# First attention regrouped: four units a step, the transposes of a group together with side work between them

## The chip, the cores and the metric

The kernel runs on one core of a Trainium2 chip. TensorE (PE, with its weight loads shown as PEld) multiplies, VectorE (DVE) and ScalarE (ACT) do the elementwise work, GpSimd (POOL) and SyncE (SP) only start transfers here. The metric is the device time of one execution, in microseconds (us). All matrices are float32. Products of weights are made of three passes over a high and a low part (`w_hi`, `w_lo`, made on ACT and DVE from each slab of weights).

## The reference

The program is a chain of three layers on 512 positions of width 1024: two blocks of a mixer and an MLP, then a hybrid layer. The change lies in the first mixer alone, a block-causal attention with 16 heads of 64:

```python
q, k, v = jnp.split(h @ w_in, 3, axis=-1)
q = rms_norm(q.reshape(B, S, A_HEADS, A_HEAD_DIM), q_gain) * (A_HEAD_DIM ** -0.5)
k = rms_norm(k.reshape(B, S, A_HEADS, A_HEAD_DIM), k_gain)
...
s = jnp.einsum('bihd,bjhd->bhij', qc, kb).astype(jnp.float32) + bias
s = jnp.where(valid[None, None, None, :], s, -jnp.inf)
p = jax.nn.softmax(s, axis=-1).astype(vb.dtype)
return jnp.einsum('bhij,bjhd->bihd', p, vb)
...
return o @ w_out
```

## The kernel before

Queries are cut in four tiles of 128. A **unit** is one head `h` and one query tile `it`; it sees the 128 x (`it`+1) positions up to its own tile, so its scores are 128, 256, 384 or 512 wide. There are 64 units, and two heads (a head pair) have eight: `it` = 0, 0, 1, 1, 2, 2, 3, 3. Each goes through this chain:

- PE scores (L651), two units back to back, into one of three PSUM banks;
- DVE adds the bias, negates and takes the row's extreme (L2016) into `a_p` and `neg_max`;
- ACT takes the exponential and the row sum (L1235);
- DVE takes the reciprocal (L2025) and scales (L2027), for two units at once;
- PE transposes the 128x128 tiles of `a_p` (L660) into bank 3 or 4;
- ACT copies them to `a_pt` (L1229);
- PE multiplies by the values (L674), two units at once, into bank 5 or 6; four such products finish the head pair `i`.

Every engine walks the same counter `s`, one unit a step: scores of unit `s`, transposes of unit `s`-6, values of unit `s`-8. On PE the order in a step is scores, transposes, values, then side work. All buffers have eight slots, `a_pt` four.

**Side work.** PE has other products to do meanwhile: the last two panels of `v` (heads 8 to 15), eight uses of 24 matmuls of 256 columns (L476), each in two bursts of 12, in bank 7, copied to `a_v` by ACT (L1209). They take slabs 10 and 11. A slab of weights is split by ACT (`w_hi`, L1088), which waits until PE has used the slab before the last, and then by DVE (`w_lo`, L1517), which waits for ACT. The slab after them (index 12, the first of the output projection) is split in step 26; the side use that frees its buffer ends in step 21. At the end of the attention PE runs the first six of the eight parts of the first output tile (`first_out`) between the last units.

**Finished head pairs.** The first four (`A_EARLY`) are copied to `a_oT` by DVE (L2036), and split to `h_hi` (ACT, L1240) and `h_lo` (DVE, L2031) in steps 41 to 44 and one step later. The last four are split straight from PSUM (L1244, L2039). DVE also does eight products of the conditioning (`ada`, L1541) on the way, one in four steps.

Each engine runs its instructions in the order in which they are written; the waits are on semaphores (`s_full`, `s_done`, `e_done`, `p_ready`, `t_full`, `pt_ready`, `o_full`, `hi_done`, `lo_done`).

Of the kernel before, what the change touches and what calls it, by code (L numbers as in the profile page):

```python
# [11 lines left out]
P = 128  # L12
T = 512
# [44 lines left out]
A_ADA = 8  # L58

# [16 lines left out]
def program(nc, I, out, tab_d, tz_d):  # L76
    ctx = ExitStack()
    with ctx:
# [258 lines left out]
        SIDE_A, SIDE_H = Side([0, 8, 14, 20, 26, 30, 34, 38], TT, 2), Side([1, 11, 22, 33, 44, 55], 2, 2)  # L337
        A_BANKS = {0: 2, 2: 1, 4: 0}
        A_OUT = 6
        A_KEPT = [41 + i for i in range(A_EARLY)]  # L340
# [8 lines left out]
        H_READ = len(SIDE_A.starts) + 1 + H_USES.index(SIDE_H.starts[-1]) + 1  # L349
        ZA_READ = len(SIDE_A.starts) + 1 + H_USES.index(SIDE_H.starts[1]) + 1  # L350
        C_COPIED = [len(SIDE_A.starts) + 1 + H_USES.index(step) + 1 for step, (i, part) in CMP_STEPS.items() if part == 1]
        SIDE_ALL = len(SIDE_A.starts) + 1 + len(H_USES)
# [108 lines left out]
        def _(pe):  # L461
# [179 lines left out]
            def attention_a(score, value, extra):  # L641

                for s in range(NUA + 7):
                    if s < NUA and s % 2 == 0:
                        if s in A_BANKS:
                            pe.wait_ge(sem("acc_free"), c("bank", -A_BANKS[s]))
                        if s >= 2:
                            pe.wait_ge(sem("s_done"), s - 1)
                        for j in range(2):
                            q, k, n = score(UNITS_A[s + j])  # L650
                            last = mm(ps[(s + j) % 3][:, 0:n], q, k, start=True, stop=True)  # L651
                        last.then_inc(sem("s_full"), 1)
                    u = s - 6
                    if 0 <= u < NUA:
                        n = P * (UNITS_A[u][1] + 1)
                        pe.wait_ge(sem("p_ready"), u + 1)
                        if u >= 2:
                            pe.wait_ge(sem("pt_ready"), u - 1)
                        for j in range(0, n, P):
                            last = nc.tensor.transpose(ps[3 + u % 2][:, j:j + P], a_p[:, u % 8, j:j + P], ident[:])  # L660
                        last.then_inc(sem("t_full"), 1)
                    u = s - 8
                    if u >= 0 and s % 2 == 0:
                        h, it = UNITS_A[u]
                        i = h // 2
                        pe.wait_ge(sem("pt_ready"), u + 2)
                        if it == 0 and i >= 2:
                            if i - 2 < A_EARLY:
                                pe.wait_ge(sem("o_kept"), i - 1)
                            else:  # L670
                                pe.wait_ge(sem("xo_lo"), i - 1)
                        for j in range(it + 1):
                            for par in range(2):
                                last = mm(ps[5 + i % 2][HD * par:HD * par + HD, it * P:(it + 1) * P], value(UNITS_A[u + par], j),  # L674
                                          a_pt[:, (u + par) % 4, j * P:(j + 1) * P], start=j == 0, stop=j == it, skip_group_check=True)
                        last.then_inc(sem("o_full"), 1)
                    extra(s)
# [109 lines left out]
            def score_a(u):  # L787
                h, it = u
# [3 lines left out]
            def value_a(u, j):  # L792
                if u in ((8, 0), (12, 0)):
                    pe.wait_ge(sem("side_free"), TT if u[0] == 8 else 2 * TT)
                return a_v[:, j, u[0] * HD:(u[0] + 1) * HD]

            def pair_a(u, k, sl):
                t, cols = u % TT, slice(k * 256, (k + 1) * 256)
                return (ps[7][:, 0:256], (w_hi[sl][:, cols], w_lo[sl][:, cols]),
                        (h_hi[:, k, t * P:(t + 1) * P], h_lo[:, k, t * P:(t + 1) * P]), True)  # L800
# [3 lines left out]
            def first_out(k):  # L804

                sl = c.base("slab") % 2
                if k == 0:
                    pe.wait_ge(sem("s_done"), NUA)
# [690 lines left out]
        def _(dve):  # L1499
# [507 lines left out]
            for s in range(8 * (KT - 1) + 17):  # L2007
# [11 lines left out]
                if SIDE_A.slab(s):  # L2019
                    split()  # L2020
# [485 lines left out]
```

## Time and profile before

| | us |
|---|---|
| median of 3 runs | 1805.32 (1804.76 to 1806.77) |
| span of the profiled execution | 1804.1 |
| first score to last value product | 156.2 to 259.7 |
| PE busy over the span | 1743.7 (97%) |
| DVE busy, ACT busy | 1174.8, 666.0 |

The page has no time of the profiled execution other than its span, from the first to the last instruction; the three times lie 0.7 to 2.7 above it. PE is busy nearly throughout, and the chain of work that ended last is PE for 80% of the span. A busy PE is not one at its peak: a row of the chain of waits gives the time that a block of matmuls held the chain, from its start to the start of what follows.

### The profile page before, as it was taken

The page shows a single profiled execution, that of the slowest core. Times are in us where ns is not written, and L with a number is a line of the kernel's source. Part 1 is how long each engine was busy: PE and PEld are TensorE (multiplying, and loading weights), DVE is VectorE, ACT ScalarE, POOL GpSimd, SP SyncE. Part 2 cuts the span into 40 slices and gives each one's busy share as a digit, 9 for nine tenths or more (in the row PEclk, how much of TensorE's full clock was granted, in tenths as well). Part 3 has the DMA queues.
Part 4 walks back from the last instruction along what each step waited for, and adds up shares of the span by engine and source line. Part 5 has one row for each costly group of instructions (what it writes and reads, how often), then busy time and mean ns, then how long its engine had stood idle before and what let it go on. Part 6 is the DMA issues. An engine that isn't in the chain of part 4 may idle for free.

```text
span 1804.1 us, 24298 instructions
## 1 busy us (share of the span) xinstructions
PE 1743.7 (97%) x9361; PEld 1440.3 (80%) x9361; DVE 1174.8 (65%) x2441; ACT 666.0 (37%) x1081; POOL 101.1 (6%) x194
## 2 busy tenths in 40 slices
PE   4999999999999999999999999999999999989999
PEld 3877769888888888888888898888888887766787
DVE  7778766876376656565454558874687478656564
ACT  4324673523242333233132335232323342366512
POOL 0001100001000100100000000010001100000000
PEclk9999999999999999999999999999999999999999
DMA  9355324335433634652423224354335322300351
GB/s 376 117 184 184 112 72 158 120 138 172 141 117 117 190 119 157 208 181 70 153 81 140 92 84 156 131 167 169 130 138 179 137 94 92 130 36 24 147 193 47
DMA packets 45471, 245.98 MB, mean 136 GB/s; under 512 B 6256, under 2 KB 6480, under 8 KB 27440
## 3 DMA queue, kind: packets, MB, share of 16 engines
q1 hardware_dynamic: 24848, 155.36, 24.0%
q0 software_dynamic: 20512, 89.11, 14.8%
q8 instruction: 74, 1.21, 0.3%
q14 instruction: 37, 0.30, 0.1%
HBM read 229.23 MB, written 15.22 MB: 135 GB/s over the span
## 4 chain that ended last, share of the span: by engine, by line
PE 80%; DVE 12%; ACT 4%; issue 2%; DMA 2%; DVEq 0%; SPq 0%; ACTq 0%
PE ps L476 69%; DVE w_lo L1517 3%; DMA ada_raw<-in_ada 1%; PE ps L840 1%; ACT w_hi L1088 1%; DVE ada_raw L1541 1%; PE ps L973 1%; DVE ada_first L1902 1%; PE ps L651 1%; DVE pre L1634 1%; PE ps L660 1%; PE ps L674 1%; PE ps L962 1%; PE ps L998 1%; PE ps L953 1%
## 5 line engine op out<-in xcount | busy, mean ns | idle before, releaser
L1517 DVE TENSOR_TENSOR w_lo<-w_raw,w_hi 128x2048 fp32r<-128x2048 f32 x136 | 311.6, 2291 | 137.3 <-ACT w_hi L1088 137.1
L1088 ACT ACTIVATE w_hi<-w_raw 128x2048 fp32r<-128x2048 f32 x136 | 260.1, 1913 | 354.3 <-PE ps L476 329.2
L476 PE MATMUL ps<-h_hi,w_hi 128*128 128x512 f32 (+1 forms) x1008 | 378.2, 375 | 5.2 <-DVE w_lo L1517 3.3
L476 PE MATMUL ps<-h_lo,w_hi 128*128 128x512 f32 (+1 forms) x1008 | 372.7, 370 | 0.0
L476 PE MATMUL ps<-h_hi,w_lo 128*128 128x512 f32 (+1 forms) x1008 | 372.5, 370 | 0.0
L476 PEld LDWEIGHTS ps<-h_hi,w_hi 128*128 128x128 f32 x1008 | 190.2, 189 | 39.8 <-issue 4.5
L476 PEld LDWEIGHTS ps<-h_hi,w_lo 128*128 128x128 f32 x1008 | 190.1, 189 | 32.1
L476 PEld LDWEIGHTS ps<-h_lo,w_hi 128*128 128x128 f32 x1008 | 190.3, 189 | 30.2
L476 PE MATMUL ps<-hid_hi,w_hi 128*128 128x512 f32 (+1 forms) x576 | 211.6, 367 | 0.0
L476 PE MATMUL ps<-hid_hi,w_lo 128*128 128x512 f32 (+1 forms) x576 | 210.9, 366 | 0.0
L476 PE MATMUL ps<-hid_lo,w_hi 128*128 128x512 f32 (+1 forms) x576 | 210.9, 366 | 0.0
L476 PE MATMUL ps<-w_hi,h_hi 128*128 128x512 f32 (+1 forms) x480 | 185.9, 387 | 16.2 <-DVE h_lo L1922 9.1
L476 PE MATMUL ps<-w_lo,h_hi 128*128 128x512 f32 (+1 forms) x480 | 183.1, 382 | 0.0
L476 PE MATMUL ps<-w_hi,h_lo 128*128 128x512 f32 (+1 forms) x480 | 182.7, 381 | 0.0
L1541 DVE CUSTOM_DVE_ANT_0 ada_raw<-ada_raw,cond 128x1024 f32<-128x1024 f32 x104 | 126.0, 1222 | 43.0 <-DMA ada_raw<-in_ada 41.9
L476 PEld LDWEIGHTS ps<-hid_lo,w_hi 128*128 128x128 f32 x576 | 108.7, 189 | 17.6
L476 PEld LDWEIGHTS ps<-hid_hi,w_hi 128*128 128x128 f32 x576 | 108.7, 189 | 17.5
L476 PEld LDWEIGHTS ps<-hid_hi,w_lo 128*128 128x128 f32 x576 | 108.7, 189 | 17.4
L476 PEld LDWEIGHTS ps<-w_hi,h_hi 128*128 128x128 f32 x480 | 92.0, 192 | 36.4 <-DVE w_lo L1517 8.2
L397 POOL DMA_DIRECT2D ada_raw<-in_ada x104 | 55.7, 536 | 971.0 <-DVE mod_s L1541 907.0
L476 PEld LDWEIGHTS ps<-w_hi,h_lo 128*128 128x128 f32 x480 | 92.1, 192 | 17.1
L1296 ACT ACTIVATE relu<-ps 128x512 f32<-128x512 f32 x56 | 33.5, 599 | 195.3 <-PE ps L476 195.0
(391 smaller groups left out, 2430.7 us busy)
## 6 DMA issues: line engine op xcount, KB each, us to landing
w_raw<-in_slabs SPq DMA_DIRECT2D x136, 1024.0 KB, 4.8
ada_raw<-in_ada POOLq DMA_DIRECT2D x104, 512.0 KB, 5.1
s_tables<-s_tab POOLq DMA_DIRECT2D x4, 2692.0 KB, 9.2
s_t<-s_tables POOLq DMA_DIRECT2D x4, 2692.0 KB, 9.8
ada_first<-in_ada SPq DMA_DIRECT2D x16, 512.0 KB, 15.1
a_bias<-in_a_bias POOLq DMA_DIRECT2D x16, 256.0 KB, 3.5
xT<-in_xT SPq DMA_DIRECT2D x4, 512.0 KB, 6.2
s_toeplitz<-KTp POOLq DMA_DIRECT2D x32, 64.0 KB, 3.2
```

Of the source, the lines that this page charges most:

```text
L397: gp.dma_start(ada_raw[:, k % 2, :], I["ada"][k]).then_inc(sem(f"ada_in{k % 2}"), 16)
L476: last = mm(o, l, r, start=start and n == 0, stop=stop and n == 2)
L651: last = mm(ps[(s + j) % 3][:, 0:n], q, k, start=True, stop=True)
L660: last = nc.tensor.transpose(ps[3 + u % 2][:, j:j + P], a_p[:, u % 8, j:j + P], ident[:])
L674: last = mm(ps[5 + i % 2][HD * par:HD * par + HD, it * P:(it + 1) * P], value(UNITS_A[u + par], j), a_pt[:, (u + par) % 4, j * P:(j + 1) * ...
L840: last = mm(b[:, t * P:(t + 1) * P], b_v[:, t, gm * P:(gm + 1) * P], b_ws[:, gm // 3, :], start=True, stop=True)
L953: last = mm(ps[(s + g) % 3][:, 0:n], hqr[r, i, ts], hk[r, br - 1, 0:n], start=True, stop=True)
L962: last = nc.tensor.transpose(ps[3 + u % 2][:, j:j + P], h_p[:, u % 8, j:j + P], ident[:])
L1088: A(w_hi[s][:], w_raw[:, s, :], ACT.Copy).then_inc(sem("hi_done"), 1)
L1296: A(relu[:, g % 2, :], b[:], ACT.Relu).then_inc(sem("relu_done"), 1)
L1517: tt(w_lo[s][:], w_raw[:, s, :], w_hi[s][:].bitcast(F32), ALU.subtract).then_inc(sem("lo_done"), 1)
L1541: V.tensor_tensor_reduce(out=w, in0=w, in1=cond[:, which, :], scale=1.0, scalar=0.0, op0=ALU.mult, op1=ALU.add, accum_out=mod_s[:, o:o + 1 ...
```

## The change

The unit of the walk becomes a **group** of four units: two heads, and the query tiles (3, 0) or (2, 1), so each group has the same ten 128x128 tiles. There are 16 groups, and the counter `s` now counts groups, 0 to 18. A step on PE is: scores of both pairs of group `s` (four banks: 4 and 5, 6 and 0); of group `s`-2 the transposes in three rounds r = 0, 1, 2 (unit, unit, and the last two units together, banks 1 and 2 in turn); between rounds 1 and 2 side work (slot 0); side work again (slot 1); then the values of group `s`-3, all into bank 3. The 16 side bursts have fixed places (`A_BURSTS`): three in step 0, three in step 1, two each in steps 2, 3 and 4, one each in 5, 6, 7 and 8, and none after that. `first_out` runs in steps 16 to 18.

ACT copies a round with one instruction, so 48 copies instead of 64, each behind an exponential of the same step. DVE takes one reciprocal for four units. The `ada` products come in steps 2 to 9. The split of slab 12 stands in step 2, the kept head pairs are split in steps 9 to 12 (`A_KEPT`), on ACT at the end of the step and on DVE at the end of the same step.

```diff
+        GROUPS_A = [(h, its) for h in range(0, A_HEADS, 2) for its in ((3, 0), (2, 1))]
+        A_SCORES, A_TURNED, A_O = ((4, 5), (6, 0)), (1, 2), 3
+        A_BURSTS = [(0, 0), (0, 0), (0, 1), (1, 0), (1, 0), (1, 1), (2, 0), (2, 1), (3, 0), (3, 1), (4, 0), (4, 1),
+                    (5, 0), (6, 0), (7, 0), (8, 0)]
+        A_DONE = [A_BURSTS[2 * u + 1][0] for u in range(A_SIDE)]
+        A_FIRST_OUT = [(16, 1), (16, 1), (17, 0), (17, 1), (18, 0), (18, 1)]
+        A_KEPT = [9 + i for i in range(A_EARLY)]
...
     PE:
-                for s in range(NUA + 7):
+                for s in range(NGA + 3):
+                    if s < NGA:
+                        h, its = GROUPS_A[s]
+                        for pair in range(2):
...
+                                pe.wait_ge(sem("s_done"), 4 * s - 2 + 2 * pair)
+                            for par in range(2):
+                                q, k, n = score(h + par, its[pair])
+                                last = mm(ps[A_SCORES[pair][par]][:, 0:n], q, k, start=True, stop=True)
+                            last.then_inc(sem("s_full"), 1)
+                    g = s - 2
+                    if 0 <= g < NGA:
+                        for r in range(3):
+                            v = 3 * g + r
+                            if r == 2:
+                                extra(s, 0)
+                            pe.wait_ge(sem("p_ready"), 4 * g + (1, 2, 4)[r])
+                            if v >= 2:
+                                pe.wait_ge(sem("pt_ready"), v - 1)
...
+                    extra(s, 1)
...
     side use u on PE:
+                    else:
+                        wait(pe, "side_free", u)
...
     ACT:
+                    for q in range(4):
+                        if s < NGA:
+                            act.wait_ge(sem("s_done"), 4 * s + q + 1)
+                            A(p, p, ACT.Exp, ...).then_inc(sem("e_done"), 1)
+                        g = s - 2
+                        if 0 <= g < NGA and q < 3:
+                            act.wait_ge(sem("t_full"), 3 * g + q + 1)
+                            A(a_pt[:, g % 2, p], ps[A_TURNED[(3 * g + q) % 2]][...], ACT.Copy).then_inc(sem("pt_ready"), 1)
+                    for u, done in enumerate(A_DONE):
+                        if done == s:
...
+                            A(a_v[...], ps[A_SPARE[u]][:, 0:256], ACT.Copy).then_inc(sem("side_free"), 1)
+                            if u == TT - 1:
+                                split()
                     if s in A_KEPT:
                         i = A_KEPT.index(s)
                         act.wait_ge(sem("o_kept"), i + 1)
                         A(h_hi[:, i, :], a_oT[:, i, :], ACT.Copy).then_inc(sem("xo_hi"), 1)
     DVE:
+                if s in (0, A_DONE[TT - 1]):
                     split()
+                g = s - 1
+                if 0 <= g < NGA:
+                    dve.wait_ge(sem("e_done"), 4 * g + 4)
+                    step(V.reciprocal(row_inv[:, m], row_sum[:, m]))
+                    for q in range(4):
+                        ts_(p, p, row_inv[:, n:n + 1], None, ALU.mult).then_inc(sem("p_ready"), 1)
-                if s - 1 in A_KEPT:
-                    i = A_KEPT.index(s - 1)
+                if s in A_KEPT:
+                    i = A_KEPT.index(s)
                     dve.wait_ge(sem("xo_hi"), i + 1)
                     tt(h_lo[:, i, :], a_oT[:, i, :], h_hi[:, i, :].bitcast(F32), ALU.subtract).then_inc(sem("xo_lo"), 1)
```

Three places show what stands in a row now. A row names line, operation, tiles and shape; the brackets are the semaphores it waits on.

**PE, a stretch without side work** (late in the stage; `ps` is a PSUM bank). Before, scores, transposes and values of two units alternate:

```order
L651 MATMUL ps0<-a_kT_96,a_qT_95 128x512 [waits s_done]
L651 MATMUL ps1<-a_kT_96,a_qT_95 128x512
L660 MATMUL ps3<-ident_62,a_p_101 128x128 [waits pt_ready,p_ready]
L674 MATMUL ps6<-a_pt_102,a_v_97 64x128 [waits pt_ready]
L674 MATMUL ps6<-a_pt_102,a_v_97 64x128 x7
L660 MATMUL ps4<-ident_62,a_p_101 128x128 [waits pt_ready,p_ready]
L651 MATMUL ps2<-a_kT_96,a_qT_95 128x128 [waits s_done]
L651 MATMUL ps0<-a_kT_96,a_qT_95 128x128
```

Now, from the last round of transposes of step 8 (the last with a side burst) to the first scores of step 9:

```order
L683 MATMUL ps1<-ident_62,a_p_99 128x128 [waits pt_ready,p_ready]
L683 MATMUL ps1<-ident_62,a_p_99 128x128
L702 MATMUL ps3<-a_pt_100,a_v_95 64x128 [waits pt_ready]
L702 MATMUL ps3<-a_pt_100,a_v_95 64x128 x9
L669 MATMUL ps4<-a_kT_94,a_qT_93 128x384 [waits s_done]
```

The four score products of a step follow each other, and the ten value products too; the last round of transposes (bank 1 again) waits for the copy of the first round.

**DVE, the split of slab 12.** Before, it stands between two units, after their scaling:

```order
L2025 RECIPROCAL row_inv<-row_sum 128x2 [waits e_done]
L2027 TENSOR_SCALAR a_p<-a_p,row_inv 128x512 [waits dve_step]
L2027 TENSOR_SCALAR a_p<-a_p,row_inv 128x512
L2016 ISA a_p,neg_max<-ps,a_bias 128x256 [waits t_full,s_full]
L2016 ISA neg_max 128x1
L1517 TENSOR_TENSOR w_lo<-w_raw,w_hi 128x2048 [waits hi_done]
```

Now, in step 2, it stands ahead of the scaling of group 1:

```order
L2074 ISA a_p,soft<-ps,a_bias 128x128
L2074 ISA soft 128x1
L1572 TENSOR_TENSOR w_lo<-w_raw,w_hi 128x2048 [waits hi_done]
L2092 RECIPROCAL soft<-soft 128x4 [waits e_done]
L2095 TENSOR_SCALAR a_p<-a_p,soft 128x384 [waits dve_step]
L2095 TENSOR_SCALAR a_p<-a_p,soft 128x384
L2095 TENSOR_SCALAR a_p<-a_p,soft 128x256 x2
L1596 ISA ada_raw,mod_s<-ada_raw,cond 128x1024 [waits ada_in0]
```

What moved is the wait for `hi_done`: the scaled tiles that PE transposes next in step 3 now come behind it.

**DVE, the low part of a kept head pair.** Before, it stands between the scores of two units:

```order
L2016 ISA a_p,neg_max<-ps,a_bias 128x256 [waits t_full,s_full]
L2016 ISA neg_max 128x1
L2031 TENSOR_TENSOR h_lo<-a_oT,h_hi 128x512 [waits xo_hi]
L2016 ISA a_p,neg_max<-ps,a_bias 128x256 [waits t_full,s_full]
L2016 ISA neg_max 128x1
```

Now, in step 12, it is the last of the step, ahead of all score rows of step 13:

```order
L2092 RECIPROCAL soft<-soft 128x4 [waits e_done]
L2095 TENSOR_SCALAR a_p<-a_p,soft 128x384 [waits dve_step]
L2095 TENSOR_SCALAR a_p<-a_p,soft 128x384
L2095 TENSOR_SCALAR a_p<-a_p,soft 128x256 x2
L2099 TENSOR_TENSOR h_lo<-a_oT,h_hi 128x512 [waits xo_hi]
L2074 ISA a_p,soft<-ps,a_bias 128x384 [waits t_full,s_full]
```

What it waits for (`xo_hi`) is the last instruction of the same step on ACT.

## Rows read from the trace of the kernel before

**Rows 1.** The page's head and first part: span; busy time of an engine.
```profile
span 1804.1 us, 24298 instructions
PE 1743.7 (97%) x9361; PEld 1440.3 (80%) x9361; DVE 1174.8 (65%) x2441; ACT 666.0 (37%) x1081; POOL 101.1 (6%) x194
```

**Rows 2.** Stretch, length, busy PE, PEld, DVE, ACT, POOL; clock, DMA, GB/s.
```profile
156.20:260.40 104.20, 101.19 (x818) 70.15 (x819) 74.23 (x258) 73.56 (x212) 11.83 (x20) 1.00 0.31 104
222.30:250.70 28.40, 27.85 (x230) 16.42 (x230) 23.51 (x91) 25.39 (x78) 2.26 (x4) 1.00 0.19 63
```

**Rows 3.** The chain of waits in the attention: start us, us, what.
```profile
199.82 0.59 PE ps L660 x4
...
201.80 1.06 PE ps L651 x4
202.86 0.26 PE ps L660
203.12 1.02 PE ps L674 x16
204.15 1.63 PE ps L476 x12
205.78 0.11 PE ps L660
205.89 1.43 PE ps L476 x12
207.31 0.42 PE ps L651 x4
...
208.10 0.37 PE ps L674 x4
```

**Rows 4.** Timeline of ACT: start us, us, engine, line, operation, [idle before].
```profile
238.48 0.60 ACT L1229 ACTIVATE a_pt<-ps 128x512 f32<-128x512 f32 x1 [0.20 <-PE ps L660]
238.98 0.60 ACT L1235 ACTIVATE a_p<-a_p,neg_max 128x384 f32<-128x384 f32 x1
...
240.29 0.72 ACT L1235 ACTIVATE a_p<-a_p,neg_max 128x512 f32<-128x512 f32 x1 [0.20 <-DVE neg_max L2016]
...
241.26 0.71 ACT L1235 ACTIVATE a_p<-a_p,neg_max 128x512 f32<-128x512 f32 x1
...
241.96 0.58 ACT L1244 ACTIVATE h_hi<-ps 128x512 fp32r<-128x512 f32 x1
...
243.51 0.40 ACT L1235 ACTIVATE a_p<-a_p,neg_max 128x128 f32<-128x128 f32 x1
```

**Rows 5.** Timeline of PE and of DVE around the widest scores.
```profile
238.38 1.13 PE L651 MATMUL ps<-a_kT,a_qT 64*128 64x512 f32 x4
...
239.55 0.69 DVE L2016 CUSTOM_DVE_ANT_0 a_p<-ps,a_bias 128x512 f32<-128x512 f32 x1 [1.27 <-PE ps L651]
...
240.98 0.75 DVE L2027 TENSOR_SCALAR a_p<-a_p,row_inv 128x384 f32<-128x384 f32 x2
```

**Rows 6.** Groups of the page's fifth part: busy us, mean ns, idle before, releaser.
```profile
L1517 DVE TENSOR_TENSOR w_lo<-w_raw,w_hi 128x2048 fp32r<-128x2048 f32 x136 | 311.6, 2291 | 137.3 <-ACT w_hi L1088 137.1
L1088 ACT ACTIVATE w_hi<-w_raw 128x2048 fp32r<-128x2048 f32 x136 | 260.1, 1913 | 354.3 <-PE ps L476 329.2
...
L1541 DVE CUSTOM_DVE_ANT_0 ada_raw<-ada_raw,cond 128x1024 f32<-128x1024 f32 x104 | 126.0, 1222 | 43.0 <-DMA ada_raw<-in_ada 41.9
```

**Rows 7.** Timeline of PE: other stages, and the attention's first scores.
```profile
42.84 0.77 PE L476 MATMUL ps<-w_hi,h_hi 128*128 128x512 f32 x1 [4.08 <-DVE h_lo L1922]
...
156.19 0.49 PE L651 MATMUL ps<-a_kT,a_qT 64*128 64x128 f32 x4 [0.52 <-DVE a_v L2000]
...
1710.02 0.50 PE L1009 MATMUL ps<-Tz,UT 128*64 128x128 f32 x2 [1.88 <-DVE v_b L2334]
```

**Rows 8.** Stretches behind those idle times, columns as in rows 2.
```profile
42.80:47.70 4.90, 4.86 (x12) 3.83 (x13) 4.80 (x9) 2.29 (x2) 0.00 (x0) 0.50 0.41 157
1710.00:1712.00 2.00, 1.98 (x10) 1.99 (x11) 0.62 (x1) 0.00 (x0) 0.00 (x0) 0.56 0.71 291
```

More of the change, by code:

```diff
@@ L58 @@
 A_ADA = 8
+GROUP = 2 * (TT + 1) * P
 SG_HALF, SG_GROUPS = 3072, 8
@@ L348, in program @@
         H_USES = sorted([*SIDE_H.starts, KCT_STEP, *U_STEPS, *CMP_STEPS])
[L349 to L352, printed above, removed]
+        H_READ = A_SIDE + 1 + H_USES.index(SIDE_H.starts[-1]) + 1
+        ZA_READ = A_SIDE + 1 + H_USES.index(SIDE_H.starts[1]) + 1
+        C_COPIED = [A_SIDE + 1 + H_USES.index(step) + 1 for step, (i, part) in CMP_STEPS.items() if part == 1]
+        SIDE_ALL = A_SIDE + 1 + len(H_USES)
         @block.sync
@@ L641, in attention_a @@
             def attention_a(score, value, extra):
-                for s in range(NUA + 7):
[L644 to L664, printed above, removed]
-                        i = h // 2
[L666 to L675, printed above, removed]
@@ L785, in _, with score_a, value_a, side_a @@
                     turn_x(p)
-            def score_a(u):
-                h, it = u
+            def score_a(h, it):
                 r = slice(HD * (h % 2), HD * (h % 2) + HD)
                 return a_qT[r, h // 2, it * P:(it + 1) * P], a_kT[r, h // 2, 0:P * (it + 1)], P * (it + 1)
[L792 to L800, printed above, removed]
+            def value_a(h, j):
+                if h in (8, 12) and j == 0:
+                    pe.wait_ge(sem("side_free"), TT if h == 8 else 2 * TT)
+                return a_v[:, j, h * HD:(h + 1) * HD]
+            def side_a(b):
+                u, part, sl = b // 2, b % 2, c.base("slab") % 2
+                if part == 0:
+                    if u % TT == 0:
+                        wait(pe, "lo_done", c("slab", 1))
+                    if u == 1:
+                        pe.wait_ge(sem("acc_free"), c("bank"))
+                    else:
+                        wait(pe, "side_free", u)
+                t = u % TT
+                for k in range(4 * part, 4 * part + 4):
+                    cols = slice(k * 256, (k + 1) * 256)
+                    last = three(ps[A_SPARE[u]][:, 0:256], (w_hi[sl][:, cols], w_lo[sl][:, cols]),
+                                 (h_hi[:, k, t * P:(t + 1) * P], h_lo[:, k, t * P:(t + 1) * P]), k == 0, k == KT - 1, weights_move=True)
+                if part:
+                    last.then_inc(sem("slab_used" if t == TT - 1 else "acc_full"), 1)
+                    if t == TT - 1:
+                        c.add("slab")
             out_bank = []
```

172 lines of the change are left out of this document (100 added, 72 removed).

## The prediction

> **What bounds the kernel now.** I read the page's head first: PE is busy for 97% of the span [rows 1], so a microsecond taken from PE's own work, or added to its waits, should move the end by one. Then the busy time by stretch [rows 2]: the changed stage, from the first scores to the sixth part of the first output tile, runs from 156.2 to 260.4, 104.2 us. PE is busy in 101.2 of them, so it idles for 3.0. ACT comes near it (25.39 of 28.40) only in the part without side work, from 222.3 to 250.7. So PE bounds the stage, and the question is what its time is made of. The chain of waits answers that [rows 3]: four score records of 512 columns take 1.06 us, four of 128 take 0.42; four transposes 0.59, one 0.26; sixteen value records 1.02, four 0.37. Each block is a slope plus a lead: scores 0.213 for 128 columns of all four records and a lead of 0.21; a transpose 0.11 and a lead of 0.15; a value record 0.054 and a lead of 0.15; a side burst 1.43 and, first in a run, a lead of 0.20 (1.63). A score or value product of the program is two records, a transpose one. The leads are what the change can take away.
>
> **PE's work.** Before, a head pair costs: scores 0.42 + 0.63 + 0.84 + 1.06 = 2.95; transposes 2 x (0.26 + 0.37 + 0.48 + 0.59) = 3.40; values 0.37 + 0.59 + 0.81 + 1.02 = 2.79 (the middle terms by the slopes). That is 9.14, times 8 head pairs 73.1. Between two bursts a transpose costs 0.11 and not 0.26 [rows 3], 0.15 less in 8 places. Side uses 8 x (1.63 + 1.43) = 24.5. That leaves 101.2 - 73.1 + 1.2 - 24.5 = 4.8 of PE's busy time for the six parts of `first_out`, three matmuls of 512 columns each. After: scores of a group have five column blocks, 5 x 0.213 + 0.21 = 1.28; transposes 10 x 0.11 + 2 leads = 1.40; values 20 x 0.054 + 0.15 = 1.23; a group 3.91, 16 groups 62.6. Side bursts 16 x 1.43 and 13 leads = 25.5. `first_out` 4.4, in four runs and not six (two leads of 0.2 less). Minus three leads for transposes between bursts (steps 2 to 4): 92.0. Before it was 101.2. **Saved: 9.2 us.** DVE takes 16 reciprocals fewer, ACT 16 copies fewer; where those engines have room PE's work hides it, and where they don't, it is in the sums below.
>
> **The waits that come.** I follow each step from the start of PE's scores. On ACT an exponential holds the engine for its duration (0.70 for 512 columns, 241.26 to 241.96; 0.60, 0.50, 0.40 for 384, 256, 128), a copy for 0.1 less than its duration (0.50 for one of 0.60, 238.48 to 238.98) [rows 4].
>
> *Step 1.* The third side use waits for `side_free` 2, the ACT copy of the second, and that stands behind the step's four exponentials. From PE's start: DVE may begin at 0.96 (scores of 384; for 512 it is 1.17, from 238.38 to 239.55 [rows 5]), the exponential 0.60 later, then 0.60 + 0.60 + 0.50 + 0.50 and the copy 0.4: 4.15. PE is there at 1.28 + 1.63 = 2.9. **1.2.**
>
> *Step 3.* Its first transposes need group 1 scaled, and that stands on DVE behind the `w_lo` of slab 12. The split can only begin when PE has finished step 2's last burst: then ACT's last copy of the use 0.35, `w_hi` 1.91, `w_lo` 2.2 (2.29 less the overlap with the next) [rows 6], reciprocal and the first scaling 0.6, signals 0.15: 5.2. PE has 1.28 of scores to do. **4.0.** Then DVE has three scalings (0.9, by the pair of 0.75 in rows 5), `ada` (1.15 [rows 6]) and the first scores (0.5), ACT an exponential (0.6) and the copy (0.5) before PE may do its third round, 3.6 after it resumed; PE's own work there is 0.8 + 1.63. **1.2.** Before, the same split made DVE wait, but with PE's next operands already scaled.
>
> *Steps 9 to 15, no side work.* The third round of transposes needs the copy of the first, which stands behind the step's first exponential: 1.17 to DVE, 0.74 more to ACT (239.55 to 240.29), the exponential 0.70 and the copy 0.60 [rows 4, 5] = 3.2; PE is there at 1.28 + 1.03 = 2.3. That is 0.9 in a step of tiles (3, 0), and 0.6 likewise with (2, 1). In steps 9 to 12 it is more: DVE's last instruction of the step waits for ACT's last. From DVE's first scores: 0.74, ACT's four exponentials and three copies (0.70 + 0.50 + 0.70 + 0.50 + 0.40 + 0.27 + 0.40 = 3.5), `h_hi` 0.62, `h_lo` 0.65: 5.5 us a step, where PE's work is 3.9. Step 9 has `ada` and the put behind that, 1.4 more. Following it: PE waits 0.6, 3.0, 1.5, 1.6, 1.4, 0.9, 0.6 in steps 9 to 15. **9.6.**
>
> *The end.* Step 16 waits 0.4 for its own copy. The last head pair is split after the last values (0.6 and 0.7 and signals, 1.5), and PE has only one part of the output tile left to cover it (0.7), where it had two. **1.2.**
>
> Together 17.2 us of waits, against the 3.0 that rows 2 show before. PE can start its scores 0.5 earlier: the first ones had waited for DVE to empty a bank [rows 7], and now have banks that are free. The stage: 92.0 + 17.2 - 0.5 = 108.7, against 104.2: **4.5 longer**; a second working, step by step in order of time, gave 3.4. I take 4.0.
>
> **The clock.** It stood at full speed, 2.4 GHz, throughout the stage [rows 2]. Elsewhere in this kernel PE idled 4.08 us and then ran 4.9 us at 0.50, which is 1.2 GHz; and once 1.88 us of idleness sufficed, with 0.56 over the next two [rows 7, 8]. Each such fall costs 1 to 2.45 us of PE's work. The waits of step 3 (4.0) and step 10 (3.0) are of this size. In step 3 the wait behind it hides 1.2 of the loss, in step 10 DVE's lateness hides 0.9. I take 1.5 for both together, bounds 0 and 4.9 (twice 2.45). The Trainium skill (TensorE: Matmul & The Clock Gate, section What's actually happening) has the throttled clock as the resting state, which activity lifts; by that rule, the trace agrees, both waits would be followed by half speed.
>
> Nothing else moves: the biases and `ada` tiles are asked for on POOL behind the same counts, and the next slab is split in time for PE.
>
> The sum is +5.5 on a span of 1804.1 that lies 1.2 below the median of the runs; the median comes to **1810.8**. Within 0.2% (3.6 us) a measurement of this kernel hardly tells a change.
>
> **Rivals.**
>
> *No fall of the clock, or a hidden one.* Then +3 to +4.5, 1808.3 to 1809.8. For it: the stage never lost the clock, and PE does some work between its waits. Against: rows 7.
>
> *The waits are not where I put them; faster.* If DVE's wait in steps 9 to 12 stays off PE's path and those steps run at PE's own work, 9.6 goes, and the clock's loss in step 10: +4.0 - 9.6 = -5.6, 1799.7. It decides from total waits under about 12 us, since 9.2 + 3.0 + 0.5 = 12.7 are what the change takes away. For it: rows 2 show ACT and DVE busy 0.89 and 0.83 in the part without side work, and PE idle for only 0.55 of 28.4. Against: the order of the three instructions is fixed, and 5.5 is a sum of rows.
>
> *The clock falls again and again.* Waits of 1.4 to 3.0 in four steps in a row; with a fall of 1.7 after each, +5.5 + 4 x 1.7 = 1817.6. The Trainium skill (same page, A second HAM failure mode: psum-queue depth-cycling) tells of a kernel whose short idle times between groups made the clock go up and down; rows 2 show none of it in the stage before, where PE's idle times were short. In the same place ends the case that the change does not do what it says: if a wait between adjacent blocks brings the lead back, 16 x (0.21 + 0.15) = 5.8 of the saving goes, 1816.6.
>
> **How the numbers follow.** The forecast (1808.9 to 1814) 0.45; no fall of the clock 0.23, a bit over half of it within 0.2%; faster 0.13; the two slow cases 0.10; a stage whose waits are some microseconds shorter than I sum, so that it ends where it was, 0.09. Slower: 0.45 + 0.10 + 0.10 = 0.65; same 0.13 + 0.09 = 0.22; faster 0.13. The range reaches from 1801.5, which takes in part of the rival below, to 1816, short of the slow ones; the likeliest case's own range is 1808.3 to 1814.
>
> **What would show it.** In the profile after: score blocks of 1.28, values of 1.23 a step; DVE's `w_lo` of step 2 idle some 5 us for `w_hi` and PE idle about 4 before transposes in step 3, the clock at 0.50 behind it; `h_lo` from `a_oT` waiting for ACT four times, and steps 10 to 13 some 5.4 long where steps 14 and 15 are about 4.7; first_out ending near 264. I am wrong if PE's idle time in the stage is below 12 us, or if the stage is shorter than 104.2.

## The result, and the profile after

The changed kernel takes 1809.07 us (median of 20 runs, 1807.98 to 1810.63), the kernel before 1805.97 in the same session. The ratio is 1.0017, 95% interval [1.0010, 1.0024]: slower by some 3 us, where +5.5 was forecast. That is less than the 0.2% within which the prediction said that a measurement hardly tells a change, but the interval is clear of 1. The first part of the page, against [rows 1]:

```profile
span 1806.6 us, 24136 instructions
PE 1735.4 (96%) x9361; PEld 1443.3 (80%) x9361; DVE 1172.3 (65%) x2425; ACT 660.9 (37%) x1065; POOL 99.9 (6%) x194
```

PE is busy for 8 us less, and the span is 2.5 longer. To measure all kernels alike I take the stage from the end of PE's work in front of the first scores to the first product of the output tile that waits for the last head pair, or, in the old order, to the same product (below: the stage). In the kernel before it holds, besides the stretch of [rows 2], the 0.52 of idle time in front [rows 7] and 0.7 of products at the end. Busy time by stretch, columns as in [rows 2], first the kernel before:

```profile
155.67:261.12 105.45, 101.93 (x822) 70.55 (x822) 75.42 (x259) 74.72 (x212) 11.83 (x20) 1.00 0.31 104
```

and the changed kernel, the stage and then five pieces of it:

```profile
154.66:263.78 109.12, 94.79 (x822) 75.18 (x821) 72.01 (x242) 69.56 (x196) 10.62 (x20) 0.95 0.29 100
154.66:178.26 23.60, 18.53 (x140) 15.50 (x139) 12.63 (x37) 14.35 (x34) 0.54 (x1) 0.97 0.32 114
178.26:183.50 5.24, 5.24 (x25) 5.24 (x26) 5.21 (x19) 2.79 (x9) 1.06 (x2) 0.50 0.88 305
183.50:223.37 39.87, 36.30 (x348) 29.45 (x347) 31.16 (x107) 25.32 (x78) 6.91 (x13) 1.00 0.37 126
223.37:228.50 5.13, 5.13 (x36) 3.32 (x36) 3.20 (x10) 3.41 (x12) 0.00 (x0) 0.67 0.00 0
228.50:263.78 35.28, 29.59 (x279) 21.67 (x277) 19.81 (x73) 23.70 (x66) 2.12 (x4) 1.00 0.15 46
```

The stage is 3.7 us longer. PE idles for 14.3 of it (109.12 less 94.79), before for 3.5, and two pieces run at a lowered clock. What PE's blocks cost now is seen where it does not wait; the chain of waits (start, us, what), to be held against [rows 3]:

```profile
156.01 4.50 PE ps L492 x36
...
164.61 3.13 PE ps L492 x24
...
196.70 1.24 PE ps L702 x20
197.94 1.28 PE ps L669 x8
199.22 1.02 PE ps L683 x8
200.25 1.44 PE ps L492 x12
201.69 0.22 PE ps L683 x2
201.90 1.24 PE ps L702 x20
```

Scores and values are what the slopes and leads gave (1.28 and 1.23). But the side burst (L492) takes 1.44 behind transposes, where I had it with a lead, 1.63, as it has behind values in [rows 3]. The same rows have it at 1.43 behind a transpose, which I took for the second of a run. Behind scores (156.01: three bursts) and behind a wait (164.61: two) one lead is there. PE's timeline, all rows with an idle time from step 3 on (the last bracket says how long, and who ended it):

```profile
178.26 1.54 PE L683 MATMUL ps<-ident,a_p 128*128 128x128 f32 x6 [3.87 <-DVE a_p L2095]
...
216.26 0.63 PE L683 MATMUL ps<-ident,a_p 128*128 128x128 f32 x4 [0.64 <-ACT a_pt L1284]
223.37 0.41 PE L683 MATMUL ps<-ident,a_p 128*128 128x128 f32 x2 [2.93 <-ACT a_pt L1284]
229.03 0.63 PE L683 MATMUL ps<-ident,a_p 128*128 128x128 f32 x4 [0.34 <-ACT a_pt L1284]
234.65 0.41 PE L683 MATMUL ps<-ident,a_p 128*128 128x128 f32 x2 [1.44 <-ACT a_pt L1284]
239.71 0.63 PE L683 MATMUL ps<-ident,a_p 128*128 128x128 f32 x4 [1.32 <-ACT a_pt L1284]
244.95 0.41 PE L683 MATMUL ps<-ident,a_p 128*128 128x128 f32 x2 [1.07 <-ACT a_pt L1284]
249.33 0.63 PE L683 MATMUL ps<-ident,a_p 128*128 128x128 f32 x4 [0.64 <-ACT a_pt L1284]
252.56 0.41 PE L683 MATMUL ps<-ident,a_p 128*128 128x128 f32 x2 [0.34 <-ACT a_pt L1284]
263.78 0.50 PE L492 MATMUL ps<-h_hi,w_hi 128*128 128x512 f32 x1 [0.53 <-DVE h_lo L2085]
```

These are steps 3, 9 to 16 and the end; with 1.20 in step 1 they make the 14.3. The six transposes at 178.26 took 1.54, with the clock at 0.50; in experiment 8, at full clock, the same row has 0.88. DVE's timeline shows what stands behind the two kinds of wait, the slab split of step 2 (L1572) and the low part of a kept pair (L2099):

```profile
175.37 2.29 DVE L1572 TENSOR_TENSOR w_lo<-w_raw,w_hi 128x2048 fp32r<-128x2048 f32 x1 [4.68 <-ACT w_hi L1132]
...
219.10 0.69 DVE L2099 TENSOR_TENSOR h_lo<-a_oT,h_hi 128x512 fp32r<-128x512 f32 x1 [0.90 <-ACT h_hi L1299]
...
225.99 0.69 DVE L2099 TENSOR_TENSOR h_lo<-a_oT,h_hi 128x512 fp32r<-128x512 f32 x1 [1.67 <-ACT h_hi L1299]
...
231.87 0.69 DVE L2099 TENSOR_TENSOR h_lo<-a_oT,h_hi 128x512 fp32r<-128x512 f32 x1 [1.15 <-ACT h_hi L1299]
...
237.28 0.69 DVE L2099 TENSOR_TENSOR h_lo<-a_oT,h_hi 128x512 fp32r<-128x512 f32 x1 [1.67 <-ACT h_hi L1299]
```

### The profile page after: what moved, and what is told of

Same layout as the page of the kernel before. It is cut to its first block, busy times and chain, and to the rows that moved or that the text cites. A ratio compares the mean times of both kernels' runs of the same rounds, so it can differ in the third digit from the quotient of the medians.

```text
span 1806.6 us, 24136 instructions
## 1 busy us (share of the span) xinstructions
PE 1735.4 (96%) x9361; PEld 1443.3 (80%) x9361; DVE 1172.3 (65%) x2425; ACT 660.9 (37%) x1065; POOL 99.9 (6%) x194
## 4 chain that ended last, share of the span: by engine, by line
PE 80%; DVE 12%; ACT 4%; issue 2%; DMA 2%; DVEq 0%; SPq 0%; ACTq 0%
PE ps L492 70%; DVE w_lo L1572 3%; ACT w_hi L1132 1%; PE ps L884 1%; PE ps L1017 1%; DVE ada_first L1957 1%; DVE pre L1689 1%; PE ps L702 1%; DMA ada_raw<-in_ada 1%; DVE ada_raw L1596 1%; PE ps L1006 1%; PE ps L1042 1%; PE ps L669 1%; PE ps L683 1%; PE ps L997 1%
## 5 line engine op out<-in xcount | busy, mean ns | idle before, releaser
L1572 DVE TENSOR_TENSOR w_lo<-w_raw,w_hi 128x2048 fp32r<-128x2048 f32 x136 | 311.6, 2291 | 141.0 <-ACT w_hi L1132 140.8
L492 PE MATMUL ps<-h_hi,w_hi 128*128 128x512 f32 (+1 forms) x1008 | 377.6, 375 | 5.7 <-DVE w_lo L1572 3.2
L492 PE MATMUL ps<-h_lo,w_hi 128*128 128x512 f32 (+1 forms) x1008 | 372.1, 369 | 0.0
L492 PE MATMUL ps<-h_hi,w_lo 128*128 128x512 f32 (+1 forms) x1008 | 372.0, 369 | 0.0
L492 PEld LDWEIGHTS ps<-h_hi,w_hi 128*128 128x128 f32 x1008 | 190.0, 189 | 40.5 <-issue 4.4
L492 PEld LDWEIGHTS ps<-h_hi,w_lo 128*128 128x128 f32 x1008 | 190.0, 188 | 32.2
L492 PEld LDWEIGHTS ps<-h_lo,w_hi 128*128 128x128 f32 x1008 | 190.1, 189 | 30.3
L492 PE MATMUL ps<-hid_hi,w_hi 128*128 128x512 f32 (+1 forms) x576 | 211.4, 367 | 0.0
L492 PE MATMUL ps<-hid_hi,w_lo 128*128 128x512 f32 (+1 forms) x576 | 210.6, 366 | 0.0
L492 PE MATMUL ps<-hid_lo,w_hi 128*128 128x512 f32 (+1 forms) x576 | 210.5, 366 | 0.0
L492 PE MATMUL ps<-w_hi,h_hi 128*128 128x512 f32 (+1 forms) x480 | 185.6, 387 | 17.5 <-DVE h_lo L1977 9.5
L492 PE MATMUL ps<-w_lo,h_hi 128*128 128x512 f32 (+1 forms) x480 | 183.0, 381 | 0.0
L492 PE MATMUL ps<-w_hi,h_lo 128*128 128x512 f32 (+1 forms) x480 | 182.7, 381 | 0.0
L492 PEld LDWEIGHTS ps<-hid_hi,w_hi 128*128 128x128 f32 x576 | 108.6, 189 | 17.6
L492 PEld LDWEIGHTS ps<-hid_lo,w_hi 128*128 128x128 f32 x576 | 108.7, 189 | 17.5
L492 PEld LDWEIGHTS ps<-hid_hi,w_lo 128*128 128x128 f32 x576 | 108.6, 189 | 17.5
L492 PEld LDWEIGHTS ps<-w_hi,h_hi 128*128 128x128 f32 x480 | 92.3, 192 | 37.3 <-DVE w_lo L1572 8.8
L492 PEld LDWEIGHTS ps<-w_hi,h_lo 128*128 128x128 f32 x480 | 92.4, 192 | 16.9
L492 PEld LDWEIGHTS ps<-w_lo,h_hi 128*128 128x128 f32 x480 | 92.4, 192 | 16.1
```

Source lines behind the costliest of these rows:

```text
L492: last = mm(o, l, r, start=start and n == 0, stop=stop and n == 2)
L1572: tt(w_lo[s][:], w_raw[:, s, :], w_hi[s][:].bitcast(F32), ALU.subtract).then_inc(sem("lo_done"), 1)
```

## The experiments

All ratios are to the kernel before as measured beside each run (1805.93 to 1806.56). The last three columns are from the one profiled execution of each kernel. "Rest" is the profiled span less the time at which the stage ends. It held 1543.0 us in the kernel before and 1542.8 in the changed one, but not in all the others, and that matters below. PE's instructions in the rest are the same in all rows, so where PE is busy there for longer, it ran at the lowered clock for longer.

| kernel | median us | ratio [95%] | stage us | rest us | PE busy in it |
|---|---|---|---|---|---|
| before | 1805.97 | | 105.45 | 1543.0 | 1515.1 |
| changed | 1809.07 | 1.0017 [1.0010, 1.0024] | 109.12 | 1542.8 | 1515.0 |
| 1 split later | 1804.61 | 0.9990 [0.9981, 0.9999] | 103.08 | 1545.3 | 1518.6 |
| 2 kept pair later | 1805.79 | 0.9996 [0.9987, 1.0005] | 106.01 | 1542.7 | 1515.1 |
| 3 both | 1800.27 | 0.9964 [0.9950, 0.9978] | 99.53 | 1545.6 | 1518.8 |
| 4 and no double burst | 1798.08 | 0.9955 [0.9942, 0.9968] | 98.06 | 1544.2 | 1517.6 |
| 5 and values first | 1798.54 | 0.9955 [0.9942, 0.9968] | 97.38 | 1544.6 | 1517.2 |
| 6 old order, split earlier | 1810.45 | 1.0021 [1.0013, 1.0030] | 109.63 | 1541.4 | 1514.3 |
| 7 filler, too long | 1810.77 | 1.0021 [1.0012, 1.0030] | 110.08 | 1545.2 | 1518.8 |
| 8 filler, sized | 1810.52 | 1.0022 [1.0013, 1.0031] | 107.67 | 1545.8 | 1517.5 |
| 9 filler, step 3 alone | 1812.86 | 1.0036 [1.0023, 1.0050] | 108.55 | 1544.2 | 1516.1 |
| 10 filler, step 10 alone | 1808.17 | 1.0016 [1.0007, 1.0025] | 108.20 | 1543.0 | 1515.5 |

**1. The slab split later.** ScalarE splits slab 12 at the end of step 3 instead of step 2, VectorE in step 4:

```
-                            if u == TT - 1:
-                                split()
+                    if s == 3:
+                        split()
...
-                if s in (0, A_DONE[TT - 1]):
+                if s in (0, 4):
```

> The changed kernel with one edit: the split of slab 12 one step later on ACT (end of step 3) and on DVE in step 4. Theory (PE waits in step 3 because the scaling of group 1 stands on DVE behind a low part that waits for ACT, which waits for PE's last side burst): the 3.87 us wait before the transposes of step 3 goes, and so does the stretch at half clock behind it (178 to 183 us). A wait of at most 0.3 stays there. The stage becomes 5 us shorter (3.9 and some 1.3 of the clock), the time 1804 against 1809.1. Rival (the wait is the ordinary length of the chain from scores to scaled tiles, whatever stands between): the wait stays at 3 to 4 us or moves to step 5, where the split now makes DVE late, and the time is within 1.5 us of 1809.1.

Measured: 1804.61, as the theory had it. The timeline of ACT and of DVE in this kernel:

```profile
179.31 1.90 ACT L1132 ACTIVATE w_hi<-w_raw 128x2048 fp32r<-128x2048 f32 x1
...
183.09 2.29 DVE L1572 TENSOR_TENSOR w_lo<-w_raw,w_hi 128x2048 fp32r<-128x2048 f32 x1
```

DVE no longer idles in front of the split (4.68 before), PE's wait of 3.87 is gone, and the stage is 6.0 shorter: 3.87, and some 2 for the clock, which does not fall there (1.00 from 178 to 184). The median fell by only 4.5: in the profiled execution the rest was 2.5 longer.

**2. The low part of a kept pair later.** In steps 10 to 13 DVE takes the low part of the pair kept one step earlier, ahead of the reciprocals, when ScalarE's high part is long there:

```
-                if s in A_KEPT:
-                    i = A_KEPT.index(s)
+                if s - 1 in A_KEPT:
+                    i = A_KEPT.index(s - 1)
```

> The changed kernel with one edit: the low parts of the kept head pairs on DVE one step later than the high parts on ACT (steps 10 to 13, after the scores of the step). Theory (steps 9 to 12 run at the pace of a loop: DVE's last instruction waits for ACT's last of the same step): PE's waits in steps 10 to 13, 2.93, 0.34, 1.44 and 1.32 us, become 0.9, 0.6, 0.9, 0.6, the clock does not fall at 223 us, and the four steps take 18.6 to 19.5 us in place of 23.4. The time is 1804.5. Rival (ACT's and DVE's sums of work bound these steps, not the wait): the steps shorten by less than 1.5 us in all, the time stays above 1807.5.

Measured: 1805.79, 3.3 less than the changed kernel, where 4.6 was expected; the stage is 3.1 shorter. Why it was less can be read from PE's timeline:

```profile
222.40 0.41 PE L683 MATMUL ps<-ident,a_p 128*128 128x128 f32 x2 [1.34 <-ACT a_pt L1284]
226.77 0.63 PE L683 MATMUL ps<-ident,a_p 128*128 128x128 f32 x4 [0.64 <-ACT a_pt L1284]
...
237.65 1.31 PE L702 MATMUL ps<-a_pt,a_v 128*64 128x128 f32 x20 [0.63 <-DVE h_lo L2091]
```

2.93 became 1.34, not 0.9, and the values of one step now wait 0.63 for the low part that was moved. The waits from step 9 to 16 sum to 7.0 (8.7 before the edit), and the clock no longer falls at 223.

**3. Both.** 

> Both edits, the split later and the low parts later. Theory (two separate stalls on different steps): the gains add, 9 to 10 us, the time is 1799.5, faster than the kernel before by 0.35%, which is what the saved leads of PE are worth once the two stalls are gone. Rival (the stalls hide one another, or DVE is then the bound in the steps between): less than 7 us together, 1802 to 1805.

Measured: 1800.27, 8.8 less than the changed kernel (9 to 10 expected). The gains add in the stage (6.0 and 3.1 alone, 9.6 together), the clock stays at full speed, and the kernel is now faster than the one before:

```profile
155.29:254.82 99.53, 90.80 (x822) 72.01 (x821) 71.61 (x242) 69.36 (x196) 10.61 (x20) 1.00 0.32 109
```

Here PE's work can be read without a disturbed clock: 90.8 us, against 101.93 before the change.

**4. No double burst in step 1.** Both cures, and the side bursts spread so that step 1 has one and steps 2 to 6 two. The split moves with them, to step 5 on ScalarE and step 6 on VectorE:

```
-        A_BURSTS = [(0, 0), (0, 0), (0, 1), (1, 0), (1, 0), (1, 1), (2, 0), (2, 1), (3, 0), (3, 1), (4, 0), (4, 1),
-                    (5, 0), (6, 0), (7, 0), (8, 0)]
+        A_BURSTS = [(0, 0), (0, 0), (0, 1), (1, 0)] + [(n, part) for n in range(2, 7) for part in range(2)] + [(7, 0), (8, 0)]
```

> The version with both cures (the slab split of weight slab 12 later, the low part of the kept pairs one step later), and besides the side products of step 1 moved out to a later step, so that no step has two bursts until step 2; the split moves with them to the end of step 5 on ScalarE and to step 6 on VectorE. Theory (step 1's wait of 1.20 us is TensorE waiting in front of its second burst for ScalarE's copy of the values, and goes when that burst stands elsewhere): 1.2 us less than with both cures, 1799.1. Rival (ScalarE is the one that is late there, and TensorE waits for it one block later instead): as with both cures, 1800.3.

Measured: 1798.08, 2.2 less than experiment 3, and the stage 1.5 shorter (1.2 expected). The wait of 1.20 in step 1 is gone and none took its place. This is the lowest median, 7.9 us under the kernel before; experiment 5 cannot be told from it.

**5. Values ahead of the third transposes.** Experiment 4 with the values moved in four steps:

```
                             if r == 2:
                                 extra(s, 0)
+                                if s in (10, 12, 14, 16):
+                                    values(s)
```

> The kernel of the run before it, and in steps 10, 12, 14 and 16 the values of group s-3 stand ahead of the third transposes of the step instead of behind them. In these steps TensorE waits 1.3, 1.1, 1.1 and some 0.3 us for the ScalarE copy of the step's earlier transposes. Theory (the values, 1.24 us of work that needs nothing from this step, fill these waits): 3.0 us less, 1796.1. Rival (the values' later sum is copied by VectorE sooner but the third transposes, and the copy that the next step's values need, come 1.24 us later, so that the wait moves to the next step): within 0.5 us of the run before.

Measured: 1798.54, within the rival's 0.5 us of experiment 4. PE's timeline shows where the wait went:

```profile
222.24 1.31 PE L674 MATMUL ps<-a_pt,a_v 128*64 128x128 f32 x20
223.48 0.44 PE L704 MATMUL ps<-ident,a_p 128*128 128x128 f32 x2
...
227.59 0.63 PE L704 MATMUL ps<-ident,a_p 128*128 128x128 f32 x4 [1.58 <-ACT a_pt L1290]
228.63 2.24 PE L674 MATMUL ps<-a_pt,a_v 128*64 128x128 f32 x20 [0.41 <-DVE h_lo L2097]
230.80 2.05 PE L688 MATMUL ps<-a_kT,a_qT 64*128 64x512 f32 x8
```

The even steps wait no more. The odd ones (11, 13, 15) wait 1.22, 1.58 and 1.07 instead of 0.64, and behind the 1.58 the clock fell: the values took 2.24 and not 1.31. So about half of the wait moved, as the rival said. All of PE's idle time in the stage is 2.0 shorter (7.54 in experiment 4, 5.56 here), but PE is busy for 1.3 longer (91.82, against 90.52 in experiment 4), and the stage gains 0.7, where the theory had 3.0. Without the fall it might have gained 2; no run shows that.

**6. The old order, the split earlier.** One edit to the kernel before, on ScalarE and VectorE alike:

```
-                if SIDE_A.slab(s):
+                if s in (0, 22):
```

> The kernel before (pairs one at a time), with one edit: the split of weight slab 12 stands at step 22 instead of 26 on ScalarE and VectorE. There ScalarE reaches it at about 189.5 us, in the middle of a dense stretch, and the VectorE part of 2.3 us stands between the two score subtractions of one item. Theory (the split costs by where it stands among the steps, as in the grouped kernel's step 3, and not by the grouping): TensorE waits, 1.5 to 4.5 us more, middle 3, 1809. Rival (the split is cheap in the old order wherever it stands, since single items give cover; it is the grouping that makes it dear): within 0.7 us of before, 1806.

Measured: 1810.45, 4.4 more than before. PE's timeline at the place of the edit, and in front of it:

```profile
162.55 1.83 PE L651 MATMUL ps<-a_kT,a_qT 64*128 64x512 f32 x4 [0.66 <-DVE neg_max L2016]
...
198.20 0.70 PE L651 MATMUL ps<-a_kT,a_qT 64*128 64x256 f32 x4 [1.89 <-DVE neg_max L2016]
```

The edit costs a wait of 1.89: the scores after the split come 4.4 us later than in the kernel before (193.81), those ahead of it (186.34 against 183.95) already 2.4. So in this execution the edit itself is worth 2.0, inside the range of the theory: where the split stands is what costs, in single units too. The 2.4 ahead of it is a fall of the clock (0.53 from 162.5 to 167.5), in a place that the edit does not touch; whether it comes in the other eleven executions was not recorded (the median of all twelve is 1.7 above the profiled one). In the kernel before, after the same idle time of 0.66 (and 0.63 in front of the scores ahead of them, where it is 0.91 here), the same scores ran at full speed:

```profile
162.57 1.13 PE L651 MATMUL ps<-a_kT,a_qT 64*128 64x512 f32 x4 [0.66 <-DVE neg_max L2016]
```

**7 to 10. Keeping the clock up.** The changed kernel with score products into a free bank in PE's long waits (no result is used); in 7 fifteen products in step 3 and eleven in step 10, in 8 eight and six, in 9 the eight alone, in 10 the six alone:

```
+                            if (s, r) in filler:
+                                free, times = filler[s, r]
+                                pe.wait_ge(sem("side_free"), free)
+                                for _ in range(times):
+                                    q, k, _n = score(0, 1)
+                                    mm(ps[7][:, 0:256], q, k, start=True, stop=True)
```

> The changed kernel with PE work added where it waits: in step 3, between the scores and the transposes, 15 score products of 256 columns (3.2 us) into the free bank 7, and 11 of them (2.3 us) in step 10 before the last round of transposes; nothing reads them. Theory on the clock (it falls because PE idles 3.87 and 2.93 us, and the half speed behind it costs part of the stage): with PE kept at work the granted clock stays at 2.4 GHz from 178 to 183 and from 223 to 228 us, six transposes behind the wait take 0.8 us and not 1.54, and the time falls by 2 to 3 us, to 1806.5, although work is added. Rival (the half clock is hidden behind the other engines' waits, so only idle time counts): the time stays within 0.7 us of 1809.1. Third (the added work ends after the wait would have): up to 1 us slower.

Measured: 1810.77, 1.7 over the changed kernel, more than the 1 us of the third case. The clock stayed up, but the filler was longer than the waits that it was to fill. PE's timeline:

```profile
175.97 6.63 PE L684 MATMUL ps<-a_kT,a_qT 64*128 64x256 f32 x30
...
222.19 5.01 PE L684 MATMUL ps<-a_kT,a_qT 64*128 64x256 f32 x22
```

By the chain of waits that is 6.47 in a wait of 3.87, and 4.94 in one of 2.93: 4.6 too much. The stage rose by only 1.0, so 3.6 of clock and waits came back.

> The changed kernel with score products into a free bank to keep TensorE busy in its two longest waits, like the earlier filler but sized by that run's trace, in which one product took 0.43 us: 8 in step 3 (3.45 us in a wait of 3.87) and 6 in step 10 (2.6 us in 2.93). No product's result is used. Theory (the waits stay as long as they were, and what the lowered clock cost behind them, some 3.6 us by the earlier filler's stage, comes back): 1805.5. Rival (the lowered clock cost 1.5 us as forecast, since the 1.2 us wait behind it returns once the clock is up): 1807.6.

Measured: the stage 107.67, 1.45 less than in the changed kernel, which is what the rival said (the wait of 1.38 comes back once the clock is up); the total 1810.52, which is what neither said. The two rows of the stage that show it, at full clock:

```profile
178.38 0.88 PE L690 MATMUL ps<-ident,a_p 128*128 128x128 f32 x6 [0.42 <-DVE a_p L2102]
182.06 0.63 PE L690 MATMUL ps<-ident,a_p 128*128 128x128 f32 x4 [1.38 <-ACT a_pt L1291]
```

The rest of the program took 3.0 us more. The busy time by stretch, far behind the stage, of the changed kernel and then of this one:

```profile
660.00:680.00 20.00, 18.43 (x119) 16.39 (x119) 13.63 (x26) 8.96 (x15) 2.09 (x4) 1.00 0.50 176
1550.00:1560.00 10.00, 9.27 (x66) 8.25 (x64) 7.85 (x8) 4.15 (x3) 0.00 (x0) 1.00 0.71 250
1580.00:1590.00 10.00, 8.65 (x52) 5.62 (x52) 9.36 (x42) 6.92 (x24) 0.00 (x0) 1.00 0.23 91
1710.00:1720.00 10.00, 8.12 (x55) 7.49 (x54) 3.07 (x9) 1.20 (x3) 0.05 (x1) 0.83 0.39 167
```

```profile
660.00:680.00 20.00, 18.44 (x106) 15.97 (x105) 13.63 (x26) 8.96 (x15) 2.09 (x4) 0.91 0.55 199
1550.00:1560.00 10.00, 7.94 (x47) 6.85 (x46) 7.25 (x8) 3.83 (x2) 0.00 (x0) 0.84 0.56 199
1580.00:1590.00 10.00, 8.73 (x47) 4.88 (x48) 9.09 (x42) 7.52 (x27) 0.00 (x0) 0.83 0.32 106
1710.00:1720.00 10.00, 8.11 (x61) 7.27 (x61) 5.50 (x14) 4.10 (x4) 0.00 (x0) 1.00 0.69 294
```

The clock fell in the stretches at 660, 1550 and 1580, where it had stood at 1.00, and did not at 1710, where it had fallen. No edit touches these places. An estimate from these rows (length times what the clock lacks of 1.00): 1.8, 1.6 and 1.7 lost and 1.7 won, 3.4 together, against the 3.0 by which the rest grew.

> The changed kernel with 8 score products into a free bank in the long wait of step 3 only (no result is used). In the run with both fillers the stretch from the first scores of the stage to the first product after it that waits for the last pair took 107.67 us, 1.45 less than in the changed kernel, and the rest of the program 3.0 more. Theory (the lowered clock behind step 3 cost 0.9 net of the 1.4 us wait that comes back, and the rest of the program is longer or shorter by some 3 us by where its own pauses lower the clock, whatever stands in this stage): the stretch 108.2 us. Total 1808.2 with the rest as in the changed kernel, 1811.2 with the rest as in the run with both. Rival (the filler costs by itself, as by delaying what ScalarE and VectorE do): the stretch at 109.1 or more.

> The changed kernel with 6 score products into a free bank in the long wait of step 10 only. Theory: the clock no longer falls at 223 us, the wait of step 11 rises from 0.34 to 1.3 us as in the run with both fillers, the stretch of the stage takes 108.5 us (0.6 less than in the changed kernel); total 1808.5 or 1811.5 by the rest of the program. Rival: the stretch at 109.1 or more.

Measured: the stage 108.55 and 108.20, both under the rivals' 109.1; the totals 1812.86 and 1808.17, with profiled executions of 1807.9 and 1805.7. In the run with the filler in step 10 alone the clock stayed up there and the wait of step 11 rose to 1.33, as the theory said. But the two gains of the stage must be read piece by piece. Up to the end of the wait in step 10 the changed kernel takes 68.7 us, this one 68.3 and the one with the filler in step 3 alone 67.8; behind it the three take 40.4, 39.9 and 40.7. So the filler of step 3 gave 0.9 (0.9 expected) and the fall in step 10 then cost 0.3 more than in the changed kernel; the filler of step 10 gave 0.5 (0.6 expected), and the other 0.4 came from step 3, where nothing was edited. PE's timeline there, in the run of step 10 alone:

```profile
178.16 0.88 PE L690 MATMUL ps<-ident,a_p 128*128 128x128 f32 x6 [3.86 <-DVE a_p L2102]
181.85 1.08 PE L690 MATMUL ps<-ident,a_p 128*128 128x128 f32 x4 [0.63 <-ACT a_pt L1291]
```

Behind the same wait the six transposes ran at full speed (0.88, not 1.54), and the clock fell only after them, so less of the step was slowed.

For step 3 the median lies 1.7 above even the higher of the two totals. Its five executions had spans of 1807.9 (the profiled one, mean clock 0.994) to 1813.0 (0.991), and where the other four lost their time was not recorded.

## Why the prediction was right, and which terms were off

The direction and the mechanism were right; the forecast of 1810.8 lies 1.7 above the median. In the one execution that the profile shows the stage grew by 3.7, with the clock in it. The terms of the forecast add up to 6.0 for it (-9.2 + 17.2 - 3.0 - 0.5 + 1.5), of which 5.5 was taken. The 2.3 between 6.0 and 3.7 are these:

- **PE's work: 9.2 predicted, 11.1 measured** (101.93 less the 90.8 of experiment 3, at full clock). The step that was too small is "side bursts 16 x 1.43 and 13 leads". Three of the 13 leads are there, behind scores and behind the wait of step 1. The other ten bursts stand behind transposes and have none: 10 x 0.20 = 2.0 too much. I had taken the lead from the burst behind values in [rows 3], and overlooked that the next burst there, at 1.43, stands behind a transpose.
- **The waits: 17.2 predicted, 14.3 measured** (from 3.0 and 3.5). Place by place: 1.2 and 1.20 in step 1; 4.0 and 3.87 in step 3; steps 9 to 15 0.6, 3.0, 1.5, 1.6, 1.4, 0.9, 0.6 and 0.64, 2.93, 0.34, 1.44, 1.32, 1.07, 0.64; the end 1.2 and 0.87. Two did not appear: the second wait of step 3 (1.2) and most of step 11's. In both PE ran at half speed just before and reached the place late. Experiment 8 shows them, with the clock up: 1.38, and 1.32 in step 11. With these the waits are 16.7, 0.5 under the forecast. Experiment 1 takes away one instruction's place, and its wait goes; experiment 2 takes away the other's, and 1.7 of the 8.7 from step 9 on go, with the fall of the clock.
- **The clock: 1.5 predicted net of hidden waits.** The lowered clock cost 4.0 of PE's time (94.79 less 90.8). It hid 1.4 and 1.0 of the waits above, which leaves 1.6; the filler of experiment 8 gave back 1.45. The bounds of 0 and 4.9 held it. By place, 0.9 for step 3 and 0.5 for step 10 (experiments 9 and 10).

So -11.1 + 10.8 + 4.0 = +3.7. The wait of 0.52 in front of the first scores [rows 7] is gone, as forecast. That PE reached this place 1.0 earlier (154.66, not 155.67) is not counted for the change: the work ahead is the same, and it ended anywhere from 154.55 to 156.38 in the profiled executions.

The faster rival fell because the idle time of DVE behind ScalarE's `h_hi` is there four times (0.90, 1.67, 1.15 and 1.67), and experiment 2 returns 3.3 of the total by moving what stands behind it. The rival of a clock that falls in four steps in a row fell too: behind the waits of 1.44 and 1.32 it stood at 1.00. So did the one of leads that come back: score blocks take 1.28 and PE's work is less than forecast, not 5.8 more. The measured 1809.07 lies in the range of the first rival (no fall, or a hidden one: 1808.3 to 1809.8), but its reason is not this rival's: the clock fell twice, and the stage lost 1.45 by it, as forecast. The number came out low for another reason, the 1.9 of PE's work. That the stage's 3.7 and the total's 3.1 lie so close together is in part luck, since the rest of the program, 1543.0 and 1542.8 in these two executions, is 2 to 3 us longer in others.

It differed by up to 4.4 us between kernels that are the same there, and the last two columns of the table say by what. PE was busy in it for 1514.3 to 1515.5 us in the kernels with a rest of 1541.4 to 1543.0, and for 1516.1 to 1518.8 in those with 1544.2 to 1545.8. In experiment 3 PE was busy there for nearly 4 longer than in the kernel before, with the same instructions (granted clock 0.99, against 1.00), and 2.6 of the 5.9 by which the stage is shorter were lost in that execution. The kernel before itself spans 1807.5 on average in the seven executions with a mean clock of 0.991 and 1801.7 in the one with 0.997. What stays open is why a pause lowers the clock in one execution and not in another, and so the size of the total within some 3 us.

## What to carry to other kernels

Regrouping work so that the bound engine switches less does save what the blocks say (11 us here), but a bigger group also makes each side instruction, put between two of its parts, block a larger piece: follow each of them, once, from what releases it to who queues behind it. An instruction with a long wait in front belongs one step later, ahead of the next dependent work, and two such moves turned +3.1 us into -5.7 here (a third of this kind was tried in the other direction: experiment 6, some 2 us dearer). When the change is worth a few microseconds in 1800, compare the changed stage in the traces as well as the totals, since a pause elsewhere may or may not cost a fall of the clock; PE's busy time over the untouched stretches shows whether it did.

## What the runs showed of the hardware

- A lead belongs to a pair of neighbours. A side burst took 1.63 behind values and 1.43 behind transposes, and three in a row behind scores 4.50, which is one lead of 0.2. Transposes behind a side burst had none either (0.22 for two, 0.44 for four). Values behind transposes, scores behind values and transposes behind scores each had theirs (0.15 to 0.21). In the rows the pairs with a lead are those where the shape in front of the operands changes (scores `64*128`, transposes and side bursts `128*128`, values `128*64`), and the pair without has `128*128` on both sides; no run tried that by itself.
- The same pause may lower the clock in one execution and not in another: after 0.66 us of idleness the widest scores took 1.13 in the kernel before and 1.83 in experiment 6, though the instructions up to there are the same and the idle times close (0.63 and 0.66, against 0.91 and 0.66). The clock fell from 2.4 to 1.2 GHz behind waits of 3.87 and 2.93 and, in experiment 5, of 1.58 with 0.41 soon after. Nor does it fall at a fixed place behind the wait: the six transposes behind 3.87 took 1.54 in the changed kernel, and behind 3.86 took 0.88 with the filler in step 10 alone, where the fall came later.
- One head's score product, repeated, took 0.216 a record of 256 columns (6.47 for 30). In the program, where the two heads of a pair alternate, four such records take 0.426 by the slope of [rows 3], half as much each. The operands of the two heads lie in different halves of the partitions; whether that is the reason no run tried.
